# Gated recurrence: six heads in one pass per level, the key inside the exponent, masked products in blocks of 64 rows

## The reference, cut to what matters

```
def step(state, inp):            # one chunk; b: sum of the log gates so far in the chunk
    b = cumsum(lf)
    decay = where(causal, exp(b[t] - b[s]), 0)
    att[t, s] = sum_d q[t, d] * key[s, d] * decay[t, s, d]
    o = att @ v + (q * exp(b)) @ state
    state = exp(b_last) * state + (key * exp(b_last - b)).T @ v
```

## Time and profile before

| what | us |
|---|---|
| median of three runs | 2537.64 (2537.55 to 2542.75) |
| the profiled execution | 2541.26 |
| its span, first to last instruction | 2538.8 |
| TensorE busy in the span | 2170.1 |
| VectorE busy in the span | 1732.7 |
| expert stage: TensorE products L1313 to L1315 | 621.7 + 607.9 + 608.1 |
| recurrence: products L2122 | 60.2 |

### The profile page before, as it was taken

One profiled execution on the slowest core, in us unless ns is written; L12 is line 12 of the kernel. 1 busy time (PEld: TensorE's weight loads), 2 busy tenths in 40 slices (PEclk: granted clock), 3 DMA queues, 4 the chain that ended last, 5 costly groups with the idle time before them and its releaser, 6 DMA issues. The chain is left out here.

```text
span 2538.8 us, 30384 instructions
## 1 busy us (share of the span) xinstructions
PE 2170.1 (85%) x9886; PEld 1718.4 (68%) x9886; DVE 1732.7 (68%) x2107; ACT 1246.2 (49%) x1393; POOL 300.2 (12%) x190
## 2 busy tenths in 40 slices
PE   4978979974999999999999999999457898775586
PEld 3756758753777777777777777777346667565565
DVE  4453531346999999999999999999563552557644
ACT  2332432313777777777777777777122433331130
POOL 0101124201011111111111111111000000000020
PEclk9998889987999999999999999999778757888888
DMA  6113023327899999999999999999451002000030
GB/s 195 33 52 115 17 75 92 99 78 271 315 371 366 368 366 366 367 366 372 367 374 363 363 369 366 368 368 364 181 145 25 1 0 68 32 25 0 25 103 38
DMA packets 201631, 522.32 MB, mean 206 GB/s; under 512 B 21942, under 2 KB 81342, under 8 KB 200300
## 3 DMA queue, kind: packets, MB, share of 16 engines
q1 hardware_dynamic: 191244, 486.25, 53.6%
q0 software_dynamic: 9504, 34.61, 3.7%
q10 hardware_dynamic: 832, 0.80, 0.1%
HBM read 500.60 MB, written 26.78 MB: 208 GB/s over the span
## 5 line engine op out<-in xcount | busy, mean ns | idle before, releaser
L1463 DVE TENSOR_TENSOR piece_lower<-piece,moe_upper 128x2048 fp32r<-128x2048 f32 x384 | 875.9, 2288 | 67.1 <-ACT moe_upper L1383 67.1
L1383 ACT CAST moe_upper<-piece 128x2048 fp32r<-128x2048 f32 x384 | 733.8, 1913 | 345.9 <-PE bank L1315 324.6
L1313 PE MATMUL bank<-moe_upper,x_hi 128*128 128x512 f32 x1536 | 621.7, 405 | 0.0
L1315 PE MATMUL bank<-moe_upper,x_hi 128*128 128x512 f32 x1536 | 608.1, 396 | 0.0
L1314 PE MATMUL bank<-piece_lower,x_hi 128*128 128x512 f32 x1536 | 607.9, 396 | 0.0
L1313 PEld LDWEIGHTS bank<-moe_upper,x_hi 128*128 128x128 f32 x1536 | 290.6, 189 | 86.5 <-issue 23.9
L1315 PEld LDWEIGHTS bank<-moe_upper,x_hi 128*128 128x128 f32 x1536 | 290.4, 189 | 68.5
L1314 PEld LDWEIGHTS bank<-piece_lower,x_hi 128*128 128x128 f32 x1536 | 291.1, 190 | 62.4
L264 PE MATMUL bank<-const,xs 128*128 128x128 f32 x96 | 21.0, 390 | 91.3 <-DVE xs L235 91.3
L1266 POOL COPY moe_dst<-row 128x1 uint32 (+1 forms) x32 | 7.1, 222 | 747.9 <-ACT moe_y L1373 747.9
L2122 PE MATMUL bank<-hg_lev,hg_left 128*128 128x128 f32 x384 | 60.2, 323 | 37.3 <-DVEq L2180 34.4
(11 more groups left out here) (492 smaller groups left out, 3743.8 us busy)
## 6 DMA issues: line engine op xcount, KB each, us to landing
piece<-in_w_exp_in_dram SPq DMA_DIRECT2D x256, 1024.0 KB, 6.9
piece<-in_w_exp_out_dram SPq DMA_DIRECT2D x128, 1024.0 KB, 8.0
combine_ys<-y_slots SPq DMA_DIRECT2D x8, 1024.0 KB, 9.2
ahead<-in_w_in_dram SPq DMA_DIRECT2D x3, 2048.0 KB, 8.3
ahead<-in_w_in_dram SPq DMA_DIRECT2D x4, 1536.0 KB, 6.7
diff_raw<-in_w_in_dram SPq DMA_DIRECT2D x8, 512.0 KB, 4.9
band_raw<-in_w_in_dram SPq DMA_DIRECT2D x8, 512.0 KB, 5.2
ahead<-in_w_in_dram SPq DMA_DIRECT2D x8, 512.0 KB, 4.8
```

The source lines that it names most:

```text
L1313: nc.tensor.matmul(to, hi[:, f, :], upper[u][:, t, cols], start=False, stop=False)
L1315: done = nc.tensor.matmul(to, lo[:, f, :], upper[u][:, t, cols], start=False, stop=f == NK - 1)
L1383: nc.scalar.copy(upper[h % SPLIT][:, :, :], ring[s][:, :, :]).then_inc(hi_ready, 1)
L1463: nc.vector.tensor_tensor(lower[s][:, :, :], ring[s][:, :, :], upper[h % SPLIT][:, :, :].bitcast(F32), ALU.subtract).then_inc(lo_ready, 1)
```

## The change

In the gates stage a new tensor `h.bk` holds b - log(key) (one more subtraction); `h.kd` is the exponential of b_last - bk, so its multiplication by the key is gone, and TensorE's transposes wait for the first exponential only.

In the recurrence the loop over units is gone: each step covers all six heads, 3 x 512 = 1536 columns. Exponents of the earlier half are m - bk, so `lev` holds both factors, is read by TensorE as both operands, and `left` and its multiplications go. Products are of 64x64 blocks with 64 channels each: 48 at a level with n of 0 to 5, the diagonal too, 24 at n = 6. Level 6 needs no mask: ScalarE copies its blocks into `att`. The others are masked into `near`, 2 x 768 columns, and copied from there into the diagonal blocks of `att` at the end, the first head of each unit by ScalarE and the second by VectorE. There are three `lev` buffers, PSUM is used in two halves of four banks, levels go from n = 6 down, and the diagonal comes first. GpSimd clears `near` and `att`.

```diff
 # gates stage
-            nc.vector.tensor_tensor(kd, b[:, :, P - 1:P].to_broadcast([P, HG_UNITS * NT, P]), b, ALU.subtract)
+            nc.vector.tensor_tensor(h.bk[:, :, :], h.b[:, :, :], h.bk[:, :, :], ALU.subtract)
+            dve.drain()
+            nc.vector.tensor_tensor(kd, b[:, :, P - 1:P].to_broadcast([P, HG_UNITS * NT, P]), bk, ALU.subtract)
             dve.drain().then_inc(arg_ready, 1)
             dve.wait_ge(edge_exp, 1)
-            nc.vector.tensor_tensor(h.kd[:, :, :], h.kd[:, :, :], h.key[:, :, :], ALU.mult).then_inc(kd_ready, 1)
...
-            nc.scalar.activation(h.kd[:, :, :], h.kd[:, :, :], ACT.Exp)
+            nc.scalar.activation(h.kd[:, :, :], h.kd[:, :, :], ACT.Exp).then_inc(kd_ready, 1)
...
 # recurrence, TensorE
+            def near_products(g, left, right):
+                to = product(g)
+                for x in range(HEAD_CHUNKS):
+                    for i in range(BLOCKS):
+                        cols = slice(x * P + NEAR * i, x * P + NEAR * i + NEAR)
+                        for m in range(2):
+                            rows = slice(HD * m, HD * m + HD)
+                            last = nc.tensor.matmul(to[NEAR * i:NEAR * i + NEAR, m, x * NEAR:x * NEAR + NEAR],
+                                                    left[rows, cols], right[rows, cols], start=True, stop=True)
+                last.then_inc(lev_ps, 1)
...
+            near_products(0, key, q)
...
+            last.then_inc(grown, 1)
+            pe.wait_ge(states_ready, 1)
+            for t, n in enumerate(LEVELS):
+                pe.wait_ge(lev_ready, t + 1)
+                if 2 <= t < FAR + 2:
+                    pe.wait_ge(far_done, t - 1)
+                elif t >= FAR + 2:
+                    pe.wait_ge(lev_done, t - FAR - 1)
+                if t < FAR:
+                    far_products(t + 1, n, lev[t % 3])
+                else:
+                    near_products(t + 1, lev[t % 3], lev[t % 3])
+            for m in range(2):
+                pe.wait_ge((first_ready, second_ready)[m], 1)
+                rows = slice(HD * m, HD * m + HD)
+                for u in range(HG_UNITS):
+                    for c in range(NT):
+                        x = u * NT + c
+                        to = product(N + 1)[:, m, x * HD:x * HD + HD]
+                        last = nc.tensor.matmul(to, att[:, m * HEAD_CHUNKS + x, :],
+                                                h.v[:, c, u * P + HD * m:u * P + HD * m + HD],
                                                 start=True, stop=c == 0)
                         if c:
-                            last = nc.tensor.matmul(to, qe[:, chunk], states[:, c - 1, rows], start=False, stop=True)
+                            last = nc.tensor.matmul(to, h.qe[rows, u, c * P:(c + 1) * P], states[rows, c - 1, u, :],
+                                                    start=False, stop=True)
                 last.then_inc(o_ps, 1)
...
 # recurrence, VectorE
+            def arguments(t):
+                n = LEVELS[t]
+                earlier, later = halves(b, n)
+                middle = earlier[:, :, (1 << n) - 1:1 << n].to_broadcast([P, ALL >> (n + 1), 1 << n])
+                to_earlier, to_later = halves(lev[t % 3], n)
+                if t >= 3:
+                    dve.wait_ge(lev_ps, t - 1)
+                nc.vector.tensor_tensor(to_earlier, middle, halves(bk, n)[0], ALU.subtract)
+                nc.vector.tensor_tensor(to_later, later, middle, ALU.subtract).then_inc(arg_ready, 1)
...
+            for t in range(N):
+                queries(t)
+                if t + 2 < N:
+                    arguments(t + 2)
+                dve.drain()
+                if t > FAR:
+                    take(t, LEVELS[t - 1]).then_inc(lev_done, 1)
+            dve.drain()
+            for m in range(2):
+                take(N, LEVELS[N - 1], slice(m, m + 1)).then_inc(lev_done, 1)
```

More of the change, by code:

```diff
@@ L2094, in _ @@
         @block.gpsimd
         def _(pool):
[L2096 to L2103, removed]
+            nc.gpsimd.memset(near[:, :], 0.0)
@@ L2105, in _ @@
+            nc.gpsimd.memset(att[:, :, :], 0.0).then_inc(zeroed, 1)
         @block.tensor
         def _(pe):
[L2107 to L2128, removed]
@@ new lines, in far_products @@
+            def far_products(g, n, both):
+                to, half = product(g), 1 << n
+                for x in range(HEAD_CHUNKS):
+                    for first in range(0, P, 2 * half):
+                        cols = x * P + first
+                        for m in range(2):
+                            rows = slice(HD * m, HD * m + HD)
+                            last = nc.tensor.matmul(to[first:first + half, m, x * half:x * half + half],
+                                                    both[rows, cols:cols + half],
+                                                    both[rows, cols + half:cols + 2 * half], start=True, stop=True)
+                last.then_inc(lev_ps, 1)
@@ L2139, in _ @@
         def _(act):
[L2140 to L2143, removed]
+            for t in range(N):
+                act.wait_ge(arg_ready, t + 1)
+                nc.scalar.activation(lev[t % 3], lev[t % 3], ACT.Exp).then_inc(lev_exp, 1)
+                if 2 <= t < FAR + 2:
+                    half = 1 << LEVELS[t - 2]
+                    act.wait_ge(lev_ps, t)
+                    act.wait_ge(zeroed, 1)
+                    for first in range(0, P, 2 * half):
+                        rows = slice(first, first + half)
+                        last = nc.scalar.copy(
+                            att[rows, :, first + half:first + 2 * half].rearrange("p (m h) t -> p m h t", m=2),
+                            values(t - 1, half)[rows])
+                    last.then_inc(far_done, 1)
@@ new lines, in queries, with take @@
+            def queries(t):
+                dve.wait_ge(lev_exp, t + 1)
+                later = halves(lev[t % 3], LEVELS[t])[1]
+                nc.vector.tensor_tensor(later, later, halves(q, LEVELS[t])[1], ALU.mult).then_inc(lev_ready, 1)
+            def take(g, n, m=slice(0, 2)):
+                dve.wait_ge(lev_ps, g + 1)
+                count = len(range(2)[m])
+                mask = k.hg_mask[:, n * NEAR:n * NEAR + NEAR].unsqueeze(1).unsqueeze(1)\
+                    .to_broadcast([P, count, HEAD_CHUNKS, NEAR])
+                return nc.vector.copy_predicated(spread(near[:, :])[:, m, :, :], mask, values(g, NEAR)[:, m, :, :])
@@ new lines, in _ @@
+            arguments(0)
+            arguments(1)
+            dve.wait_ge(k.mask_in, 16)
+            dve.wait_ge(zeroed, 1)
+            take(0, DIAGONAL)
+            dve.wait_ge(grown, 1)
+            added = k.psum[:, 2048:2048 + (NT - 1) * HG_UNITS * HD].rearrange("p (c u e) -> p c u e", u=HG_UNITS, e=HD)
+            nc.vector.tensor_copy(states[:, 0, :, :], added[:, 0, :, :])
+            for c in range(1, NT - 1):
+                dve.drain()
+                decay = h.eb[:, :, c * P + P - 1:c * P + P].to_broadcast([P, HG_UNITS, HD])
+                nc.vector.tensor_tensor(states[:, c, :, :], states[:, c - 1, :, :], decay, ALU.mult)
+                dve.drain()
+                last = nc.vector.tensor_tensor(states[:, c, :, :], states[:, c, :, :], added[:, c, :, :], ALU.add)
@@ L2488, in constants @@
     c[:, C_P + 2] = np.arange(P) + SLOTS + 1
[L2489 to L2492 removed]
+    row, col = p % NEAR, np.arange(NEAR)[None, :]
+    mask = np.zeros((P, NEAR_LEVELS + 1, NEAR), np.int32)
+    mask[:, NEAR_LEVELS] = row == col
+    for n in range(NEAR_LEVELS):
+        mask[:, n] = ((row ^ col) >> n == 1) & (col > row)
     n = 511 - np.arange(512)
```

165 lines of the change are left out of this document (65 added, 100 removed).

## The result

| | median, us | runs |
|---|---|---|
| before | 2539.6 | 2537.55 to 2542.75 (4) |
| changed kernel | 2470.46 | 2463.91 to 2480.76 (4) |

The ratio is 0.9734, 95% interval 0.9709 to 0.9759: 69 us faster, where 2467 (2452 to 2486) was forecast. The profiled execution took 2471.41 us, its span 2469.6. The changed kernel's runs scatter over 17 us. In a second profile of it the whole recurrence started 15 us earlier, while the stage kept its length within 0.5 us; so the scatter arises ahead of it, and in what follows stages are compared by their length in the profile.

A forecast was written before the change was run, and what follows sets the result against it. VectorE was taken to pace the recurrence: opening 10.2, levels 26.4, output 19.4 and clock 2 made 58.0 us instead of 127.4. With 1.5 off the gates, 2541.3 became 2470.4, or 2467 as median; range 2452 to 2486.

The forecast's parts named there:

- The pace: Recurrence levels: VectorE sets the pace, 4.4 us per level of all heads, 26.4 us for the levels.
- the widths: VectorE in the recurrence: 0.87 us for 768 columns, 1.68 for a masked copy of 1536 columns.
- Block products: TensorE in the levels: products on different row halves run together, 2.6 us per level at full clock, ends 5.0 and 1.3.
- Rival A: Recurrence: block products do not pair or loads stand bare, 5.0 us per level, 13 more, 2480; chance 0.18.
- Opening: Start of the recurrence: diagonal 5.2 us at 1.2 GHz, state products 3, then dependent state instructions; 10.2 us in all.
- Output: End of the recurrence: ScalarE's copies 1.9, 42 output products 9.3, division changes 7.2, last copy 1.0; 19.4 us.
- the clock: Late parts of the recurrence that TensorE sets: not all at 2.4 GHz, 2 us added.
- 36 changes: Output row: products with 128 and 64 rows alternate, 0.2 us per change of the array's division, 7.2 us.
- Rival B: Output: TensorE at 1.2 GHz throughout, the row doubles, 14 to 16 us more, 2482; chance 0.10.
- Gates: Gates stage: TensorE's transposes start 1.4 to 2.6 us earlier; 1.5 us less taken, the least 0.
- 378 x 0.28 + 16.5 + 4: Threshold, 0.28 us per block, of a recurrence rival: every block changes array division at 0.35 us, 27 slower, 2564; chance 0.03.
- (D): Output: the switches cost their least and the clock is full, 7 us less, 2460; chance 0.12.

The follow-up runs named there:

- key_mult: Changed kernel with the multiplication by the key back, one VectorE instruction of 768 columns per level: stage 68.3 us, ratio to before 0.9745.
- rows_apart: Changed kernel with a level's block products reordered so that neighbours share rows and columns of TensorE's array: stage 99.2 us, one run.
- quarters: Changed kernel with output products cut into 64x64 blocks straight from `near`, level-6 and state parts beside the last masked copies: stage 42.5 us, ratio 0.9644.
- warm: Changed kernel with twelve 128x128 filler products in the gap ahead of the output: output 21.3 us, stage 58.2, ratio 0.9690.
- the four kernels: Changed kernel repeated, with state products padded to 128 rows, with twelve filler products, with both: output 23.6, 17.3, 21.3, 9.6 us.
- full_warm: Changed kernel with state products padded to all 128 rows and twelve filler products ahead of the output: output 9.6 us, stage 47.5, ratio 0.9658.
- cols_only: Changed kernel with a level's block products reordered so that neighbours alternate column halves and keep the same rows: stage 69.2 us, one run.

## Why the prediction was right, point by point

**The pace.** Right. Levels forecast at 4.4 us and 26.4 up to the first heads' last masked copy; measured 4.53, and 2282.16 to 2308.54 = 26.4. `key_mult` shows that VectorE decides. The masked copy's pitch was 1.77 and not 1.68. The rows of 1536 columns behind the widths are multiplications (L2067, L2069) and not subtractions; it did no harm, since both have a pitch of 0.87 at 768 columns.

**Block products.** The mechanism was right and the size too dear: besides the two row halves, the two halves of the output run together too, the forecast's low end (1.3 forecast, 1.63 measured). Rival A is out. Its premise, that blocks may not overlap, costs 38 us in this stage when an order makes it true (`rows_apart`, its low clock included), and then the change would have kept 28 of its 66 us.

**Opening.** 10.2 forecast, 7.8 measured. The diagonal came at full clock (1.63, not 5.2), and GpSimd's clearing did not slow VectorE, although its copy had the earlier trace rows. The clearing cost 0.5 all the same: the first masked copy waited for it, and in `quarters`, where 3072 of its 4608 columns are gone, the opening is 7.2.

**Output.** This is the step that failed in size. Forecast 19.4 and 2 for the clock; measured 2308.54 to 2335.37 = 26.8. Term by term: ScalarE's copies 1.7 (1.9), products at full clock 9.6 (9.3), 36 changes 6.3 to 7.5 (7.2), last copy 1.0 (1.0), the clock 7.7 instead of 2. That the changes came out near 7.2 is luck: the forecast's 0.2 was meant at full clock, where `warm` shows 0.14, 5.0 for 36; the half clock brought the rest. "The outputs before ran at full clock, so I take 2" carried a clock over from products that stood between full 128x128 bursts to a row behind 64x64 bursts and an idle 2.8 us, with changing divisions; the four kernels show that it takes fillers and even products together to keep it. Rival B, given 0.10, named what happened, but doubled the changes with the rest (14 to 16); a change costs 0.14 at full and 0.18 at half clock, so it does not double.

**Gates.** 1.5 forecast, 2.7 measured; the table load did start under the subtraction, the better of the two cases that the prediction named.

**Sum.** Opening -2.4, levels 0, output +5.4: 61.0 for 58.0. Gates -1.2, drift -0.4, tail +0.25. The profiled execution lost 69.9 us against 70.9 forecast. Inside the stage errors of opposite sign, 2.4 and 5.4, partly cancelled, and the gates covered another 1.2. So the mechanism of the levels was right, and that the total came so close is luck. Nothing outside the two stages moved by more than 0.4 us within the span. Two sums in the rivals are off: 378 x 0.28 + 16.5 + 4 is 126.3 and not 127.4, and (D) with the least switches (3.6 less) and a full clock (2 less) makes 5.6 and not 7; neither changes the forecast.

## What to carry to other kernels

Where blocks of 64 rows and 64 columns alternate over all four quarters of TensorE's array, 48 float32 products take 1.63 us at full clock; in an order that leaves neighbours on one quarter they took 9.4 at half, and single-quarter neighbours at full clock still cost more than three times as much per record. So write out which quarter each neighbour uses. Do not mix products of all rows and of half the rows product by product: pad or cut until all have one shape, and count what the padding adds elsewhere (1.0 us of opening here). When several units are joined into one pass, their outputs line up at the end with nothing beside them, and what used to be hidden there is the new bound; read the granted clock there anew.

## What was not expected of the hardware

- TensorE at a granted clock of 0.50 from 2266.8 to 2389.7 us in `rows_apart`, busy 41.8 of 45 us in the stretch shown. Being busy did not raise the clock; 64x64 products with no overlap did not either, nor did those of `cols_only` (0.50, busy 31.1 us of the 34.7 of its levels). In `full_warm` even products of 128 rows behind 128x128 fillers held 1.00. What exactly the clock follows stays open.
- The output products of `warm` fell to half clock 5 us into a gapless row with alternating divisions; those of `full_warm`, all of one division, did not within 9.6 us. Each is one profile.
- GpSimd's clearing (1.38 us for 1536 columns, 2.65 for 3072) costs VectorE nothing beside it, while its copy of 512 columns had doubled a subtraction (0.82 for 0.43).
